# Third weight buffer used for expert 5 as well as expert 2, and one load of layer 0 issued earlier

## The reference

```python
def moe(x, r_w, r_b, w1, w3, w2):
    ...
    for e in range(N_EXPERTS):                       # 16 experts
        h = jax.nn.silu(t @ w1[e]) * (t @ w3[e])     # 1024 -> 512, twice
        out = out + gates[:, e:e + 1] * (h @ w2[e])  # 512 -> 1024
```

## The kernel before

| expert | 0 | 1 | 2 | 3 | 4 | 5 | 6 | 7 | 8 | ... | 15 |
|---|---|---|---|---|---|---|---|---|---|---|---|
| buffer before | 0 | 1 | third | 0 | 1 | 0 | 1 | 0 | 1 | ... | 0 |

## Time and profile before

### The profile page before, as it was taken

The page is one execution under the profiler, slowest core; times in us unless marked ns, Lnnn a source line. Parts: engine busy times, 40 slices in busy tenths (PEclk is TensorE's granted clock), DMA queues, the critical chain, the costliest instruction groups (busy, mean ns, idle before and its releaser), DMA issues.

```text
span 1018.4 us, 14233 instructions
## 1 busy us (share of the span) xinstructions
PE 935.0 (92%) x4702; PEld 464.8 (46%) x4703; DVE 340.8 (33%) x815; ACT 166.7 (16%) x337; POOL 109.5 (11%) x198
## 2 busy tenths in 40 slices
PE   6999999899999999888999999999889999998993
PEld 4666545433343333334666754554533433333331
DVE  0975455512221222216214543305612212212125
ACT  1000051110011001102213332310111110111100
POOL 0260100200111011003300033000111100111000
PEclk9999999699999999999999999999789999999997
DMA  7866584787989999987502302485487499999971
GB/s 182 234 213 206 170 339 166 295 342 235 380 318 385 374 375 397 422 300 278 157 20 83 124 25 91 181 323 202 154 337 272 150 376 389 392 405 394 424 325 52
DMA packets 74614, 266.96 MB, mean 262 GB/s; under 512 B 7528, under 2 KB 39300, under 8 KB 66353
## 3 DMA queue, kind: packets, MB, share of 16 engines
q1 hardware_dynamic: 64112, 237.74, 62.5%
q10 hardware_dynamic: 5057, 16.15, 4.5%
q0 software_dynamic: 5392, 12.34, 4.4%
HBM read 259.78 MB, written 7.15 MB: 262 GB/s over the span
## 4 chain that ended last, share of the span: by engine, by line
PE 73%; DMA 15%; DVE 6%; ACT 3%; issue 1%; SPq 1%; DVEq 0%; ACTq 0%
PE bank L1037 18%; DMA w<-in_e_w 14%; PE bank L1045 7%; PE bank L911 4%; PE bank L800 4%; PE wide L800 3%; PE wide L1080 3%; PE bank L816 3%; PE wide L911 3%; PE wide L1894 3%; PE bank L1027 2%; PE bank L1756 2%; PE bank L1724 2%; PE wide L1933 1%; PE wide L1708 1%
## 5 line engine op out<-in xcount | busy, mean ns | idle before, releaser
L1037 PE MATMUL bank<-w,dbuf 128*64 128x512 f32 x960 | 216.5, 604 | 17.1 <-DMA w<-in_e_w 14.8
L1037 PEld LDWEIGHTS bank<-w,dbuf 128*64 128x64 f32 x960 | 71.0, 139 | 159.0 <-issue 159.0
L1045 PE MATMUL bank<-w,dbuf 128*64 128x512 f32 x480 | 110.7, 604 | 2.4 <-DVE dbuf L1490 2.4
L1495 DVE COPY dbuf<-bank 64x512 f32<-64x512 f32 x64 | 44.0, 688 | 159.1 <-PE bank L1045 158.6
L1486 DVE TENSOR_TENSOR dbuf<-dbuf,bank 64x512 f32<-64x512 f32 x32 | 22.1, 690 | 204.0 <-ACT dbuf L718 204.0
L718 ACT ACTIVATE dbuf<-bank 64x512 f32<-64x512 f32 x32 | 18.9, 590 | 392.4 <-PE bank L1037 392.4
L1080 PE MATMUL wide<-dbuf,ukT 128*128 128x512 f32 x128 | 63.0, 617 | 3.0 <-DVE dbuf L1495 3.0
L1045 PEld LDWEIGHTS bank<-w,dbuf 128*64 128x64 f32 x480 | 34.2, 138 | 63.3 <-issue 61.6
L556 POOL COPY idx_col<-idx 64x1 int32 (+1 forms) x32 | 6.0, 188 | 518.6 <-PE bank L1027 347.9
L543 POOL DMA_DIRECT2D w<-in_cache_kpe x64 | 34.3, 536 | 207.8 <-PE wide L1850 91.3
L800 PE MATMUL bank<-xT,dbuf 128*128 128x320 f32 x128 | 37.2, 451 | 2.7 <-DMA dbuf<-in_a_w_pw 2.7
(11 more groups left out here) (367 smaller groups left out, 1151.5 us busy)
## 6 DMA issues: line engine op xcount, KB each, us to landing
w<-in_e_w SPq DMA_DIRECT2D x90, 2048.0 KB, 17.0
dbuf<-in_a_w_pw SPq DMA_DIRECT2D x16, 512.0 KB, 8.1
w<-u_rows SPq DMA_DIRECT2D x32, 142.0 KB, 3.0
dbuf<-in_a_w_pw ACTq DMA_DIRECT2D x4, 1024.0 KB, 6.3
dbuf<-in_e_w SPq DMA_DIRECT2D x2, 2048.0 KB, 18.7
w<-in_cache_ckv SPq DMA_DIRECT2D x32, 128.0 KB, 3.5
dbuf<-in_cache_ckv SPq DMA_DIRECT2D x32, 128.0 KB, 2.2
dbuf<-in_b_w_o SPq DMA_DIRECT2D x2, 2048.0 KB, 8.4
```

What stands on the lines that cost most here:

```text
L1037: last = nc.tensor.matmul(bank[n * C:(n + 1) * C], xe[:, k, s * C:(s + 1) * C], w[n][k], start=(k == 0), stop=(k == KD - 1))
L1045: last = nc.tensor.matmul(bank[n * C:(n + 1) * C], h[:, k], w[k][:, n * 512:(n + 1) * 512], start=(k == 0), stop=(k == 3))
L1495: last = V.tensor_copy(y_pair[s * C:(s + 1) * C, h * 512:(h + 1) * 512], DOWN[h * C:(h + 1) * C, :])
```

## The change

It touches SP's program and TensorE's. Expert 5 of each layer is loaded into the third buffer, by a new function `third_over`, bound to expert 2; experts 6 and 7 are bound to experts 3 and 4 instead of 4 and 5 and change buffers; from expert 8 on each expert is bound to the one two before it, as it was. In layer 0 `third_dbuf(0, 0)` moves from behind `mix_done` to behind expert 0's loads, with a wait for the eighth gate block.

| expert | 0 | 1 | 2 | 3 | 4 | 5 | 6 | 7 | 8 | ... | 15 |
|---|---|---|---|---|---|---|---|---|---|---|---|
| buffer after | 0 | 1 | third | 0 | 1 | third | 0 | 1 | 0 | ... | 1 |

```diff
+            def third_over(l, e, old):
+
+                served = sp.value_load(rounds[0:1, 2, old:old + 1], min_val=1, max_val=ROUNDS_MAX + 1)
+                w3, w2_all = w13_rows(l, 1, e), w2_rows(l, e)
+                sp.wait_ge(up_done, old + (E * l + 1))
+                sp.wait_ge(m_up, served)
+                sp.dma_start(third_w1, w13_rows(l, 0, e)).then_inc(w13_ready[2], 16)
+                sp.dma_start(third_w3a, w3[:, 0:5]).then_inc(w13_ready[2], 16)
+                sp.dma_start(third_w3b, w3[:, 5:8]).then_inc(w13_ready[2], 16)
+                sp.wait_ge(down_done, old + (E * l + 1))
+                sp.wait_ge(m_down, served)
+                sp.dma_start(third_w2a, w2_all[:, 0:3]).then_inc(w2_ready[2], 16)
+                sp.dma_start(third_w2b, w2_all[:, 3:4]).then_inc(w2_ready[2], 16)
+
             def load_rest(l):
                 sp.wait_ge(cnt_set, l + 1)
                 load_over(l, 3, 0, 0)
                 load_over(l, 4, 1, 1)
-                with sp.Fori(0, (E - 6) // 2) as it:
+                third_over(l, 5, 2)
+                load_over(l, 6, 0, 3)
+                load_over(l, 7, 1, 4)
+                with sp.Fori(0, (E - 8) // 2) as it:
                     for s in range(2):
-                        e = it * 2 + s + 5
-                        load_over(l, e, s, it * 2 + s + 3)
-                load_over(l, E - 1, 0, E - 3)
+                        load_over(l, it * 2 + s + 8, s, it * 2 + s + 6)
 
             load_13(0, 0, 0)
             load_2(0, 0, 0)
+            sp.wait_ge(h_done, KD)
+            third_dbuf(0, 0)
             sp.wait_ge(u_turned, 4)
             load_half(0, 1, 1, 0)
             sp.wait_ge(u_stored, 32)
             load_2(0, 1, 1)
             sp.wait_ge(mix_done, 3)
             load_half(0, 1, 1, 1)
-            third_dbuf(0, 0)
             third_dbuf(0, 1)
...
-            n1, n0 = 16 * 8 * l, 16 * 7 * l
+            n2 = 16 * 7 * l
...
-            expert(2, 0, 2, 48 * (l + 1), 32 * (l + 1), 1)
-            with pe.Fori(0, (E - 4) // 2) as it:
-                expert(it * 2 + 3, 1, 0, it * 32 + (2 * n1 + 64), it * 16 + (n1 + 32), it + 1)
-                expert(it * 2 + 4, 0, 1, it * 32 + (2 * n0 + 64), it * 16 + (n0 + 32), it + 2)
-            expert(E - 1, 1, 0, 2 * n1 + 256, n1 + 128, E // 2 - 1)
+            expert(2, 0, 2, 96 * l + 48, 64 * l + 32, 1)
+            expert(3, 1, 0, 2 * n2 + 64, n2 + 32, 1)
+            expert(4, 0, 1, 2 * n2 + 64, n2 + 32, 2)
+            expert(5, 1, 2, 96 * l + 96, 64 * l + 64, 2)
+            with pe.Fori(0, (E - 8) // 2) as it:
+                for s in range(2):
+                    expert(it * 2 + s + 6, s, s, it * 32 + (2 * n2 + 96), it * 16 + (n2 + 48), it + 3)
+            for s in range(2):
+                expert(E - 2 + s, s, s, 2 * n2 + 224, n2 + 112, E // 2 - 1)
```

More of the change, by code:

```diff
@@ L1149, in pe_experts @@
             turn_half(0, 1, UP)
-            expert(0, 0, 0, 2 * n1 + 32, n1 + 16, 0)
-            expert(1, 1, 1, 2 * n0 + 32, n0 + 16, 0)
-            expert(2, 0, 2, 48 * (l + 1), 32 * (l + 1), 1)
-            with pe.Fori(0, (E - 4) // 2) as it:
-                expert(it * 2 + 3, 1, 0, it * 32 + (2 * n1 + 64), it * 16 + (n1 + 32), it + 1)
-                expert(it * 2 + 4, 0, 1, it * 32 + (2 * n0 + 64), it * 16 + (n0 + 32), it + 2)
-            expert(E - 1, 1, 0, 2 * n1 + 256, n1 + 128, E // 2 - 1)
+            expert(0, 0, 0, 2 * n2 + 32, n2 + 16, 0)
+            expert(1, 1, 1, 2 * n2 + 32, n2 + 16, 0)
+            expert(2, 0, 2, 96 * l + 48, 64 * l + 32, 1)
[7 more added lines that the diff above has]
+                expert(E - 2 + s, s, s, 2 * n2 + 224, n2 + 112, E // 2 - 1)
             put_rows(p0 + E // 2 - 1, stop=True)
```

## The result

The changed kernel takes 1028.37 us (median of 17 runs, 1022.17 to 1035.31) against 1022.67 us for the kernel before (17 runs beside them, 1016.85 to 1025.41). The ratio is 1.0067, with a 95% interval of 1.0049 to 1.0085: **slower by 0.7%**, where 1018.0 was forecast. Its times also scatter more widely than those of before.

What follows compares the result with a forecast made beforehand. Weight transfers falling behind in the late experts were taken to cost 6.8 us in layer 0 and 10.4 in layer 1. Terms of -3.1 and +0.6 gave -2.5 us from 1020.46, hence 1018.0; range 1010.5 to 1021.5.

Steps and rivals of the forecast that it cites:

- (4): TensorE's written-out experts and shorter loop: the first branch back stays, now behind expert 7; 0 change, bounds -1.0 and +1.0 per layer.
- Rival D: Slower through instruction supply: some five more first passes per layer, 10 us added if each stalls, 1028; chance 0.07.
- (1): Layer 1, expert 5 in the third buffer: more lead at expert 8, 3.1 us gained; bounds nothing and 10.4.
- the sum: All terms together over both layers: -3.1 + 0.6 = -2.5 us, taken from the median of 1020.46.
- (2): Layer 0, the same buffer change: no gain, about 0.6 us lost as expert 8 starts from an empty queue; bounds 0 and 1.7.
- (3): Layer 0, expert 2's first matrix loaded some 50 us earlier: cost 0, at most 5 us.
- Rival A: Layer 1 keeps all the recovered lead to expert 15: 9.8 us gained, time 1011.3; chance 0.22.

Runs made afterwards that it cites:

- unroll_only: Kernel before, with only TensorE's program written out as in the change (experts 3, 4, 5, 14, 15), buffers and loads as before; 1028.37 us, ratio 1.0069.
- early_only: Kernel before, with only the load of expert 2's first matrix in layer 0 moved behind expert 0's loads; 1023.34 us, ratio 0.9998.
- after_pad198: The changed kernel with 198 never-run instructions added to TensorE's further-round code of layer 0's expert 0; 1024.18 us, ratio 1.0020.
- after_pad72: The changed kernel with 72 never-run instructions added to TensorE's further-round code of layer 0's expert 0; 1024.31 us, ratio 1.0033.
- after_short: The changed kernel without TensorE's code for further rounds in experts that have none with these inputs; 1016.15 us, ratio 0.9947.
- unroll_short: Kernel before, with TensorE's experts written out as in the change, but without further-round code where unused; buffers and loads as before; 1022.72 us, ratio 1.0015.
- reuse_only: The changed kernel without the early load of expert 2's first matrix in layer 0; 1023.45 us, ratio 1.0030.

## Why the prediction was wrong

**The step that failed** is (4), "TensorE's program writes out experts 3, 4 and 5, and the last two ... I leave it at 0 change (bounds -1.0 and +1.0 in each layer)". It measured +6 us of the medians: `unroll_only`, +6.3 over before, three times the 2.0 us of both bounds together. Two things were wrong in it. First, the instruction: I had put the stall of before down to the loop's branch back. That branch (L1153) took 0.23 us at most; the long one is the jump over expert 4's unused code, and each expert written out brings one more such jump that is taken for the first time (the same jump took 0.21 to 0.22 us in the loop's later passes):

```profile
L1095 PEldq COMPARE_BRANCH  x1: 3132/3132/3132, 824.8 to 824.8; - x1
...
L1153 PEldq COMPARE_BRANCH  x12: 76/208/228, 271.9 to 982.5; - x12
```

Second, the price: of these 3.1 us only 0.81 showed as idle time, the rest was hidden by matmuls under way. I had priced a stall by that remainder, 1.0 us. In `early_only`, which has the same TensorE program, the same jump took 4.58 us and 2.42 of it showed, and the stalls of the change run to 3.5 us. To some of them 1.6 to 1.7 us at the lower clock come: 17.3 us between experts 6 and 7 in place of 15.7. One profiled execution had shown a cheap case of an event whose cost varies.

Of the 10.4 us between forecast and result, 2.2 are no error of the mechanism: the time before was 1020.46 us from three runs and is 1022.67 from 17.

**Rival D** had the right mechanism, at a chance of 0.07, and the wrong evidence against it: "experts 0 to 2 are written out already, and no wait of this kind stands behind them". That holds for one placement of the code. In the change such a wait stands in expert 1 of layer 1, in `after_pad198` ahead of expert 1 and in `after_pad72` in expert 2 of layer 0. Its count was wrong too: not some five stalls of 1.0 us in each layer but one or two in each, of up to 4.5. That its sum, 1028, is the measured time is therefore luck.

**(1), the third buffer in layer 1**, was right in mechanism and about right in size. Expert 5 was issued at 799.38, 7 us after the start of expert 2's products as worked out; the DMA was full until 844 and half idle from 846 to 862; expert 8 was issued at the end of expert 6's products. The stage loses 6.3 us in `after_short` against 10.4 before, 4.1 gained for the 3.1 of the sum. Within the change itself it is hidden by the stalls, which also feed it: while TensorE stands, the transfers catch up.

**(2), layer 0**, was right: no gain. The loss of 0.6 us was not seen; 138.5 us in both `unroll_short` and `after_short`. (The pace of 132.4 us that both layers are held against is 132.5 by its own terms, 4 x 29.2 + 15.7; the difference changes nothing here.)

**(3), the early load**, was right for the load alone: 0.9998. Beside the rest of the change `reuse_only` leaves it open.

**Rival A** (all of the lead kept, 9.8 us) did not come, as the waits of experts 11 to 14 in `after_short` show: 5.4 us in four. By the medians the transfers' part is larger than the sum, 6.6 against 2.5 us (`unroll_short` against `after_short`); the two traces show 5.2 of it in layer 1, where `unroll_short` takes 143.9 us from expert 6 to expert 15. So the sum's term for layer 1 was low by 1 to 2 us, since layer 1 without stalls loses 11.5, and not the 10.4 that the one profile showed. What the rest of the 6.6 is was not settled.

**A rule that I had passed over.** The Trainium skill, "Runtime: NRT & Kernel Launch", Instruction fetch mechanics, says that instructions come in blocks by a DMA queue, fetched ahead in sequence only, and that a taken branch beyond the blocks at hand has to wait for its target. The trace agrees: the profile's page has that queue (q8), its packets land in the stalls, the jump itself lasts up to 5.3 us in the change, and padding moves the stalls. It also says that kernels therefore prefer full unrolling; here the runs differ, since the jumps stayed in the written-out experts, and more code with the same jumps was slower by 6 us.

What stays open: which placements stall. The places in the seven layouts that were profiled with all of their code do not follow from the position in the program by any rule that I could find, and with one and the same TensorE program the same stall differs in length (0.81 us before, 2.42 in `early_only`).

## What to carry to other kernels

Writing out the passes of a loop is not free when each carries code that is usually jumped over: count the instructions that are skipped, and compare a version with that code left out before judging what the change was meant to do. A change of layout can hide a gain of 6 us or feign a loss of 7; padding that never runs is a cheap control. Where a wait is put down to nothing, look at the engine's branches and at the packets of the instruction queue before guessing which jump it was. And read the lead of a prefetch at the point where the old binding takes over again: only what is left of it there reaches the end.

## What the runs showed of the hardware that I had not expected

The code fetch depends on the load of the DMA engines: ahead of the same expert the same TensorE program, with 47 instruction packets in both kernels, stalls for 0.17 us at 103 GB/s of traffic and for 3.44 us at 388 GB/s. A jump over unused code takes 0.2 to 0.5 us when the code behind it is there, and up to 6.5 us when it is not (`after_pad198`). An idle time of 1.99 us was enough to lower TensorE's clock once (expert 11 of layer 1: 8.78 us for products of 7.04), while a wait of 2.73 us in layer 0 left it (7.09 us for expert 13's), and so did the stall of 3.44 us (7.09 for expert 8's); the length of the idle time alone does not decide it.
